# Projecting the first four feature tiles of the queries and keys between the modulation rows

## The reference

```
mod_x = silu(c) @ ada_w + ada_b                 # 6 x 1024 numbers, 12 rows of 512
sh1, sc1, g1, sh2, sc2, g2 = split(mod_x, 6)
mod_c = silu(c_ctx) @ ada_w + ada_b             # the same for the context
hx = rmsnorm(x, norm1_g) * (1 + sc1) + sh1      # x: 512 x 1024
px = hx @ w_in                                  # 512 x 2976
fx, qlx, kvlx, krx, gx = split_proj(px)         # widths 512, 256, 128, 32, 2048
hc = rmsnorm(ctx, norm1_g) * (1 + csc1) + csh1  # ctx: 256 x 1024; pc = hc @ w_in
```

## Time and profile before

| | |
|---|---|
| median of three runs | 1675.29 us (1674.95 to 1679.92) |
| profiled execution, its own time | 1681.15 us |
| its span, first to last instruction | 1679.3 us |
| PE busy in the span | 1622.9 us (97%) |
| DVE, ACT, POOL busy | 1269.9 (76%), 924.2 (55%), 256.4 us (15%) |
| mean granted clock of TensorE, as a share of the full one | 0.986 |
| share of PE in the chain that ended last | 88% |

### The profile page before, as it was taken

One profiled execution on the slowest core, in us unless ns is written; L12 is line 12 of the kernel. 1 busy time (PEld: TensorE's weight loads), 2 busy tenths in 40 slices (PEclk: granted clock), 3 DMA queues, 4 the chain that ended last, 5 costly groups with the idle time before them and its releaser, 6 DMA issues.

```text
span 1679.3 us, 20446 instructions
## 1 busy us (share of the span) xinstructions
PE 1622.9 (97%) x8356; PEld 1330.7 (79%) x8356; DVE 1269.9 (76%) x1457; ACT 924.2 (55%) x1071; POOL 256.4 (15%) x176
## 2 busy tenths in 40 slices
PE   6999999989999999999999999999999999999994
PEld 3768876658988989899888677878888888888883
DVE  6554866877667747475799874599999999999994
ACT  6433235443444535352533234588888888888884
POOL 0000021000037332310000200102122122121200
PEclk9999999999999999999999999899999999999997
DMA  9206822004131323231222101399999999999993
GB/s 383 80 0 251 299 87 76 0 0 151 51 126 67 134 76 126 76 126 51 101 76 76 50 26 56 145 386 408 375 380 376 377 369 361 371 378 364 384 359 114
DMA packets 54484, 322.92 MB, mean 192 GB/s; under 512 B 12529, under 2 KB 13041, under 8 KB 17778
## 3 DMA queue, kind: packets, MB, share of 16 engines
q1 hardware_dynamic: 42192, 304.76, 47.6%
q0 software_dynamic: 9216, 8.43, 2.2%
q10 hardware_dynamic: 2978, 8.37, 1.3%
HBM read 323.60 MB, written 23.07 MB: 206 GB/s over the span
## 4 chain that ended last, share of the span: by engine, by line
PE 88%; DMA 3%; DVE 3%; ACT 3%; issue 1%; POOL 0%; SPq 0%; ACTq 0%; POOLq 0%; DVEq 0%
PE ps L585 25%; PE ps L1465 19%; PE ps L1492 10%; PE ps L1093 7%; PE ps L775 5%; PE ps L1017 3%; PE ps L751 2%; PE ps L1349 2%; PE ps L1449 1%; PE ps L809 1%; DMA xT<-in_x 1%; ACT whi L1543 1%; PE ps L881 1%; DMA sum_scratch<-xN 1%; PE ps L1474 1%
## 5 line engine op out<-in xcount | busy, mean ns | idle before, releaser
L2211 DVE TENSOR_TENSOR wlo<-raw,whi 128x2048 fp32r<-128x2048 f32 x256 | 584.2, 2303 | 131.1 <-ACT whi L1543 130.9
L1543 ACT ACTIVATE whi<-raw 128x2048 fp32r<-128x2048 f32 x256 | 485.5, 1911 | 152.7 <-PE ps L1465 36.9
L1465 PE MATMUL ps<-whi,xH 128*128 128x512 f32 x512 | 202.7, 396 | 0.0
L1465 PE MATMUL ps<-whi,xL 128*128 128x512 f32 x512 | 200.2, 391 | 0.0
L1465 PE MATMUL ps<-wlo,xH 128*128 128x512 f32 x512 | 199.3, 389 | 0.0
L585 PE MATMUL ps<-hH,whi 128*128 128x512 f32 x352 | 138.8, 394 | 0.3 <-ACT dmax L2024 0.3
L585 PE MATMUL ps<-hH,wlo 128*128 128x512 f32 x352 | 137.1, 390 | 0.0
L585 PE MATMUL ps<-hL,whi 128*128 128x512 f32 x352 | 137.1, 389 | 0.0
L3257 POOL DMA_INDIRECT sum_scratch<-yb,idt x32 | 51.1, 1596 | 451.6 <-ACT yb L2151 446.0
L1465 PEld LDWEIGHTS ps<-whi,xL 128*128 128x128 f32 x512 | 96.1, 188 | 20.7
L1465 PEld LDWEIGHTS ps<-wlo,xH 128*128 128x128 f32 x512 | 96.3, 188 | 19.2
(11 more groups left out here) (522 smaller groups left out, 3545.6 us busy)
## 6 DMA issues: line engine op xcount, KB each, us to landing
raw<-in_experts SPq DMA_DIRECT2D x192, 1024.0 KB, 7.9
raw<-in_streamed SPq DMA_DIRECT2D x92, 1024.0 KB, 4.9
xT<-in_x SPq DMA_DIRECT2D x1, 2048.0 KB, 17.2
h_scratch<-hN ACTq DMA_DIRECT2D x4, 512.0 KB, 2.6
sum_scratch<-xN ACTq DMA_DIRECT2D x1, 2048.0 KB, 13.3
out<-Y SPq DMA_DIRECT2D x4, 512.0 KB, 2.7
ctxT<-in_ctx SPq DMA_DIRECT2D x1, 1024.0 KB, 20.1
Y<-sum_scratch SPq DMA_DIRECT2D x2, 512.0 KB, 5.7
```

The source lines that it names most:

```text
L1465: ins = e.matmul(b.t[:, :], l, w, start=(kk == 0 and i == 0), stop=(kk == 7 and i == 2))
L1543: e.activation(u.hi, u.raw, ACT.Copy).then_inc(*p.inc("hi", n, on="hi"))
L2211: e.tensor_tensor(u.lo, u.raw, u.hi.bitcast(F32), ALU.subtract).then_inc(*p.inc("lo", n, on="lo"))
```

## The change

In SP's queue the loads of units 8 and 9 come directly behind x, and units 4 to 7 behind them. ACT and DVE convert unit 8, then 9, before units 4 to 7, and compute feature tiles 0 and 1 before the conversion of the rest (DVE), or between units 5 and 6 (ACT); tiles 2 and 3 follow singly. On PE, `spread(0)` and a shorter `fill` (9 in place of 17) come directly behind `mod_columns(0)`, then tiles 0 and 1, the first half of row 3, tile 2, the second half of row 3 and all of row 1, then tile 3 with `mod_columns(1)` inside it, and tiles 4 to 7. `norm_x` and `normed` are made to work with one tile at a time.

```diff
@@ PE, stage norm1
         total(0)
         mod_columns(0)
-        mod(3)
         spread(0, 512, ("dve", "ns", 0, 7), hold=True)
-        mod(1, (0,))
-        mod_columns(3)
-        mod(1, (1,))
...
-        def first(k):
+        def first(k, between=None):
             if k == 0:
-                fill(bs[0], 17)
+                fill(bs[0], 9)
...
             for b, (key, mw, u, m0, _) in zip(bs, heads_):
+                if between and m0:
+                    between()
+                    between = None
...
-        for k in range(8):
+        first(0)
+        first(1)
+        mod(3, (0,))
+        first(2)
+        mod(3, (1,))
+        mod(1, (0,))
+        mod_columns(3)
+        mod(1, (1,))
+        first(3, lambda: mod_columns(1))
+        for k in range(4, 8):
             first(k)
-            if k == 0:
-                mod_columns(1)
@@ ACT, stage norm1
-        convert(4)
+        convert(8)
         row(0)
         root(0)
+        convert(9)
+        convert(4)
         convert(5)
+        rounded(0, range(2), T, lambda d: modc[:, d, 0:1], lambda d: hH[:, d, :])
         convert(6)
         convert(7)
+        rounded(0, range(2, 3), T, lambda d: modc[:, d, 0:1], lambda d: hH[:, d, :])
         row(3)
-        convert(8)
-        convert(9)
-        rounded(0, range(2), T, lambda d: modc[:, d, 0:1], lambda d: hH[:, d, :])
+        rounded(0, range(3, 4), T, lambda d: modc[:, d, 0:1], lambda d: hH[:, d, :])
         row(1)
-        rounded(0, range(2, 4), T, lambda d: modc[:, d, 0:1], lambda d: hH[:, d, :])
@@ DVE: normed, norm_x, stage norm1
-            tail(d1 - 2)
-            tail(d1 - 1)
+            for d in range(max(d0, d1 - 2), d1):
+                tail(d)
...
-            p.wait_ge(*done("dve", "A1", d0, 1))
+            p.wait_ge(*done("dve", "A1", d0 // 4 * 4, 1))
...
-        convert(4)
+        convert(8)
         inverse(0)
         mod(0)
+        convert(9)
+        norm_x(0, 2)
+        convert(4)
+        norm_x(2, 3)
         convert(5)
         convert(6)
         convert(7)
-        convert(8)
+        norm_x(3, 4)
         mod(3)
         scale(4)
-        convert(9)
-        norm_x(0, 4)
         mod(1)
@@ SP
-        for n in range(4, 10):
+        for n in (8, 9, 4, 5, 6, 7):
             load(n)
```

## The result

| | before | after |
|---|---|---|
| median, seven runs each on one chip | 1678.34 us (1674.95 to 1679.92) | 1684.52 us (1681.28 to 1686.55) |
| ratio after / before, 95% interval | | 1.0034 [1.0022, 1.0046] |
| same pair, a second set of runs | | 1.0024 [1.0014, 1.0035] |
| profiled execution, its own time | 1681.15 us | 1683.4 us |
| its span | 1679.3 us | 1681.6 us |

The change makes the kernel slower, by 0.2 to 0.3%. The two profiled executions differ by only 2.25 us, the medians of the two sets of runs by 4 to 6 us; that gap is the subject of the experiments. One later run of the kernel before took 2574.28 us at a mean granted clock of 0.594; it is in none of the ratios, means and ranges here.

A forecast was written before the change was run, and what follows sets the result against it. PE was taken to bound the kernel, so the Fourier branch's start moves the end: +1.4 us from order and waits plus 1.7 us from a clock fall, +3.1 on 1675.29, gives 1678.4 us, range 1674.0 to 1682.0.

The forecast's parts named there:

- The two early tiles: Feature tiles 0 and 1 on PE: tile 0 starts at 36.0 in place of 46.50, both done at 41.6 us.
- Loads: SP's loads in the new order: unit 8 lands at 22.8 us, ACT wants it near 25.8, so no cost.
- The wait ahead of tile 2: PE idles 3.4 us, from 43.5 to 46.9, because tile 2's rounding queues behind unit 7's conversion on ACT.
- DVE's lo halves and the wait ahead of tile 4: Units 5 to 7 queue behind tile 2's tail on DVE; tile 4's tail comes late and PE waits 1 us.
- The second fall of the clock: After PE's idle ahead of tile 2, near 48 us, half clock for 3.4 us: 1.7 us of work lost.
- The mark: Start of the Fourier branch, where the feature tiles' matmuls end: from 69.55 us to near 72.6, +3.1 us.
- Rival (c): Unit 7 doesn't hold up tile 2, which starts at 43.5; Fourier branch starts at 67.6, −2 us; 8%.
- The mark moves by +1.4 us: Fourier branch's start goes from 69.55 to 70.9 us by PE's new order and waits, before the second fall's loss.
- Rival (b): Clock stays low long in both places, the fills and from the wait ahead of tile 2 on: +6.3 us; 17%.
- the prediction's other sum: Whole kernel: the shift of +3.1 us set on the profiled execution's own time, 1681.15 to 1684.3 us.

The follow-up runs named there:

- e1: Changed kernel with one line moved: on ACT the rounding of tile 2 stands ahead of unit 7's conversion; ratio to the kernel before 0.9990.
- e2: Changed kernel plus 13 unused products on ones in PE's wait ahead of tile 2; ratio to the kernel before 1.0023.
- a_before: The kernel before run again with no edit, for a second profile and the scatter of equal programs; ratio 1.0002.
- e3: Changed kernel plus unused products on ones, 8 ahead of the spread and 13 ahead of tile 2; ratio to the kernel before 1.0007.

## Why the prediction was wrong

It said 1678.4 us, 1674.0 to 1682.0, and no change that can be told. It was 1684.5 us and slower. Point by point, against the first profile of the changed kernel:

- **The two early tiles**: forecast 36.0, measured 35.33; done at 41.6, measured 41.1. The spread, the fills and the clock's return were nearly as worked out.
- **Loads**: no cost, as said. Unit 8 was there when ACT came to it.
- **The wait ahead of tile 2**: 3.4 us forecast, 3.46 measured, by the very chain (unit 7's place, ACT's queue, DVE's tail). `e1` shows it as the cause: one line moved, and the mark is 5.3 us earlier.
- **DVE's lo halves and the wait ahead of tile 4**: 1 us forecast, 0.84 measured.
- **The second fall of the clock**: 1.7 us forecast, 1.5 measured by `e2`'s profile. All three profiles of the changed kernel have it.
- **The mark**: 72.6 forecast, 72.65 in the profile. Rival (c), in which unit 7 does not hold up tile 2, put it at 67.6; `e1`, which takes that hold away, has it at 67.39.

What failed is the step "The mark moves by +1.4 us", and under it the reading of the earlier trace rows that the kernel before spends 6.9 us of its start at half clock. I took that low stretch as the kernel's own, while the first one of the changed kernel was given the short length. In two of three profiles of the kernel before the stretch was of 3.4 us and the mark 1.4 to 1.65 us earlier. So the reference point of the sum lay too late; set against the mean mark of 68.5, the change of the mark is +4.5 us. The term was mis-sized, not its mechanism: with 68.5 in place of 69.55 the same sum gives 72.6 − 68.5 = 4.1 us. Rival (b) was made of the same piece, but at the wrong end: it let the clock stay low longer after the change, not shorter before it.

The second failure is the base. The sum was put on the median of three runs, 1675.29 us. The 92 later runs of the kernel before (80 beside the variants, 12 as `a_before`) have a mean of 1679.2 us and reach from 1673.9 to 1683.0. The profiled execution lay 5.9 us above the median of the three; this was seen and not used. That the prediction's other sum, 1681.15 to 1684.3 us for the profiled execution, ends near the measured median is luck: it adds a shift that is too small to a time that lay high among those of its kernel. Of the 6.1 us between 1678.4 and 1684.5, some 3.9 are this base and 2.0 the shift (5.1 us in the means, 1684.3 − 1679.2, against 3.1; the rest is that the measured number is a median).

How the 5.1 us divide can be estimated from the runs, since each lists its span and its mean granted clock: (1 − clock) times span is an estimate of the time lost to the low clock. It counts the low clock while PE has nothing to do as well: in every profile the clock is at half for the last 20 us, behind PE's last product, and that is some 10 us of each figure. The mean is 23.2 us before (92 runs) and 26.1 us after (19 runs); what is left is 1656.0 and 1658.2 us. So 2.9 us are clock, give or take 1, and 2.1 us are waiting. Ahead of the mark the three profiles of each show 2.3 and 4.0 us lost, 1.7 of the 2.9; the remaining 2.8 us of the mark's 4.5 are waiting. The other 1.2 us of low clock lie behind the mark, where the falls near 230, 370, 935 to 970 and 1060 to 1090 us come in different numbers and lengths in every profile. The time from the mark to the end is nevertheless the same in the mean; whether the changed kernel really draws longer falls there, or three profiles are too few, is not settled.

All six profiles of the two kernels have the first fall, between 29.4 and 31.1 us, with 1.44 us (before) or 2.25 us (after) as the longest wait near it. The Trainium skill ("TensorE: Matmul & The Clock Gate", section "Why this matters for your kernels"), by which waits this short would not bring the clock down, differs from these traces; the measurement decides.

## What to carry to other kernels

When work is moved ahead on one engine, look at what then stands behind each wait on the others: here the conversion of unit 7 waited for a use that the change had moved back, and a rounding that PE needed at once stood behind it. One line in ACT's order was worth 5 us of the mark. Before a sum of a few microseconds is set against a profile, compare that profile's granted clock and time with the runs. If its time lies high among them, part of its loss is a draw and not the kernel's, and a slowdown that is worked out against it can come out too small. A base of three runs is no base for 0.2%.

## What the runs showed of the hardware

Equal programs differ by how often and how long TensorE's clock is at half. In all thirteen profiles the low stretches were of 3.4, 6.8 or 10.2 us, but for the one at the end, behind PE's last product, which lasts 19.2 to 21.0 us to the end of the span; and the same kernel had 3.4 or 6.8 us at the same place. The kernel before ranged over 9 us in its 92 runs, 0.5% of its time, without any change in its instructions. Most of that goes with the clock: the standard deviation is 2.3 us for the times and 1.0 us for what is left when (1 − clock) times span is taken off.

A fall can follow waits of under half a microsecond. In `e3` PE waited 0.37 us ahead of the sums of squares and 0.29 us ahead of the columns of row 0. It did only these small products between and behind them, and then the unused ones without a gap. The clock fell at 28.6 us, before any longer wait, and was back at 32.0:

```profile
26.82 1.05 PE L696 MATMUL ps<-oneD,sqs 128*128 128x1 f32 x8 [0.37 <-DVE sqs L2338]
28.17 0.41 PE L652 MATMUL ps<-cst,rowbuf 4*128 4x4 f32 x4 [0.29 <-ACT rowbuf L1572]
28.50 3.68 PE L624 MATMUL ps<-one 128*128 128x128 f32 x16
...
28.00:29.00 1.00, 0.83 (x6) 0.82 (x7) 1.00 (x1) 1.00 (x3) 0.00 (x0) 0.79 0.96 401
```
